# Where three activation buffers and three small tables lie in SBUF, in a two-block transformer kernel on one core

## The chip, the core and the metric

The program runs on one core of a Trainium2 chip. The metric is the device time of one execution in microseconds (us), as the median of several runs. Everything is held and computed in float32. Weights and activations that meet in a matmul are split into a high and a low part in a reduced format (`float32r`), and a product is made of three matmuls.

## What is computed

Two transformer blocks follow each other on 256 tokens of width 1024. The parts that matter here are the projections, all of them products of an activation with a large weight. In short:

```
# first block, two layers
for i in range(2):
    h = rmsnorm(x, mix_norm[i])
    p = h @ a_in   (layer 0: gated short convolution)  |  h @ b_in   (layer 1: stick-breaking attention)
    x = x + concat(y_main, y_mem) @ w_o[i]
    h = rmsnorm(x, ffn_norm[i])
    x = x + (silu(h @ w_gate[i]) * (h @ w_up[i])) @ w_down[i]       # inner width 2816
# second block: gated linear attention and spatial gating, context of 256 tokens
z = modulated_norm(x) @ w_in
x = x + g1 * ((sigmoid(ga) * (a @ w_br_a) + sigmoid(gb) * (ob @ w_br_b)) @ w_o)
x = x + g2 * ((gelu(conv3x3(h @ w_up_a)) * (h @ w_up_v)) @ w_down)   # inner width 2816
```

## The kernel before, in words

All weights come from one stream in HBM, cut into tiles of 128 x 1024 values. A tile is loaded into one of six `raw` buffers by the SyncE queue (L353), ScalarE makes its high part in one of four `w_hi` buffers (L889), and VectorE, or in the last stage GpSimd for half of the tiles, makes its low part in one of four `w_lo` buffers (L1411, L2111). TensorE then uses the tile in one of three ways:

- `tall` (L393): eight slices of 128 x 128 of the tile are the stationary operand, one after another; the moving operand is an activation of 256 columns, `H`, `Y`, `CX` or `HP`, and `mm3` (L381) makes three matmuls for each slice: high weight by high activation (L382), high by low (L383), low by high (L384). So a tile is 24 matmuls.
- `down` (L522): the same three matmuls for each of eight slices, with the moving operand `G`, one chunk of the hidden layer of a feed-forward stage. `G` has two sets that alternate.
- `wide` (L404): a slice of `H`, `Y` or `CX` is stationary, and the weight tile moves, with 256 or 512 columns (L387).

Each of `H` and `Y` is a pair of buffers, high and low, of 8192 bytes in each of the 128 partitions; the four `G` buffers have 1024 bytes each, a weight tile 4096. In the second block `H` and `Y` change names: `H2` is `Y`, `Y2` is `H` (L305). `CX` (the context's activation) and `HP` (258 columns, for the first two chunks of the last feed-forward stage) lie over the end of `ARENA`, the large work buffer; `W2S`, `CTX_LR` and `X_LR` belong to a small matmul in `log_decays` (L620), where a 96 x 256 activation moves over 96 x 128 weights.

Small tables are `MOD` (48 x 2 values, 384 bytes in a partition), which holds the modulation vectors, `GS` (3 x 8 values, 96 bytes), the scaled gains, and `small` (64 values, 256 bytes), for maxima, sums and statistics. VectorE and ScalarE read and write them.

SBUF is given out in the order of the `sb` calls of `build` (L209 to L249), without gaps but for rounding a buffer's size up to 32 bytes. Two calls make buffers that nothing uses: `phase` ahead of `H` and `whole` behind `G`, of `HALF_LINE` = 16 values, 64 bytes, each. The order of work on every engine is written out by hand, with semaphores between the engines; the places of the buffers don't enter into it.

Of the kernel before, what the change touches and what calls it, by code (L numbers as in the profile page):

```python
# [8 lines left out]
P = 128  # L9
D = 1024  # L10
KC = D // P
# [9 lines left out]
NMOD = 48  # L21
# [5 lines left out]
STACK = 96  # L27
EPS = 1e-6
RING = 4
HALF_LINE = 16  # L30
RAW = 6

F32 = mybir.dt.float32
# [163 lines left out]
def norm_low(tag, k):  # L197
    return ("norm_lo_dve", tag, k)
# [7 lines left out]
def build(nc, table, stream, vec, xT, memT, ctxT, c_rows, sq_consts, masks, scan_mask, sgu_bc, sgu_wT, gla_w2, out):  # L206
    pe, act, dve, pool, sp = nc.tensor, nc.scalar, nc.vector, nc.gpsimd, nc.sync
    with ExitStack() as ctx:
        def sb(name, shape, dt=F32):  # L209
            return ctx.enter_context(nc.sbuf_tensor(name, shape, dt))  # L210
# [5 lines left out]
        w_hi = [sb(f"w_hi{r}", [P, D], F32R) for r in range(RING)]  # L216
        w_lo = [sb(f"w_lo{r}", [P, D], F32R) for r in range(RING)]
        X = sb("X", [P, KC, T])
        sb("phase", [P, HALF_LINE])
        H = (sb("H_hi", [P, KC, T], F32R), sb("H_lo", [P, KC, T], F32R))  # L220
        Y = (sb("Y_hi", [P, KC, T], F32R), sb("Y_lo", [P, KC, T], F32R))
        G = [(sb(f"G_hi{i}", [P, T], F32R), sb(f"G_lo{i}", [P, T], F32R)) for i in range(2)]
        sb("whole", [P, HALF_LINE])
        SQ = sb("SQ", [P, KC, T])
        RS = sb("RS", [P, 2, T])
        GF = sb("GF", [P, T])
# [1 line left out]
        mask_sb = sb("mask_sb", [P, 3, P], U32)  # L228
        scan_m = sb("scan_m", [P, T])
        V = sb("V", [P, VEC_N])  # L230
        MOD = sb("MOD", [P, NMOD, 2])
        GS = sb("GS", [P, 3, KC])
        CROW = sb("CROW", [P, D])
        EPS_COL = sb("EPS_COL", [P, 1])[:]
        small = sb("small", [P, 64])
        W2 = sb("W2", [P, 512])
        LR = sb("LR", [P, T])
        CTX_LR = sb("CTX_LR", [P, T], F32R)
# [12 lines left out]
        def area(at, *shape):  # L251
            n = int(np.prod(shape))
            assert at + n <= 24832
            v = ARENA[:, at:at + n]
            if len(shape) == 1:
                return v
            names = "abc"[:len(shape)]
            return v.rearrange(f"p ({' '.join(names)}) -> p {' '.join(names)}",
                               **{names[i]: shape[i] for i in range(1, len(shape))})
# [14 lines left out]
        EXS, PTS = [area(8448, 8, T), area(11392, 8, T)], [area(10496, 4, 512), area(13440, 4, 512)]  # L274
        Y_MEM = [Y, H]
        NB = 3 * P
# [27 lines left out]

        H2, Y2 = Y, H  # L305
        RS_COLS = small[:, 32:34]
# [6 lines left out]

        SH1, SC1, G1, SH2, SC2, G2 = (lambda c, b=0, k=k: MOD[:, 8 * k + c, b:b + 1] for k in range(6))

# [56 lines left out]
        def pe_program():  # L372
# [8 lines left out]
            def mm3(o, wh, wl, xh, xl, start, stop):  # L381
                pe.matmul(o, wh, xh, start=start, stop=False, skip_group_check=True)  # L382
                pe.matmul(o, wh, xl, start=False, stop=False, skip_group_check=True)  # L383
                return pe.matmul(o, wl, xh, start=False, stop=stop, skip_group_check=True)  # L384
# [34 lines left out]
            def project(stage, count, h, release, side=None, ready=None, steps=1, order=range(KC)):  # L419
                assert n == AT[stage], (stage, n)  # L420
                for i in range(count):
                    b = bank_of(n)
                    claim(b)
                    tall(PS[:, b, 0:T], h, ready if i == 0 else None, order=order)
                    emptied[b] = [release(i)]
                    if side:
                        side.step(steps)

            def project_tokens(stage, width, h, banks, release, side, steps=1):
                assert n == AT[stage], (stage, n)  # L430
                claim(*banks)
                for part in range(KC * width // D):
                    wide([PS[:, b, 0:width] for b in banks], h, width, part)
                    if part == KC * width // D - 1:
                        for b in banks:
                            emptied[b] = [release]
                    side.step(steps)
# [84 lines left out]
            def down(l, j):  # L522
# [6 lines left out]
                for c in range(KC):  # L529
                    w = slice(c * P, (c + 1) * P)  # L530
                    last = mm3(PS[:, 4 + c // 2, (c % 2) * T:(c % 2 + 1) * T], w_hi[r][:, w], w_lo[r][:, w],
                               G[j % 2][0][:], G[j % 2][1][:], j == 0 and c % 2 == 0, j == FC - 1)
                    if j == FC - 1 and c % 2 and c != KC - 1:
# [216 lines left out]

            H_of = [H, H2, H2]

            def launch_norms():
                quarters("mix0", CSQ, 5)
                yield
                quarters("mem0")
                sum_quarters("mix0", 5)
                yield
                sum_quarters("mem0")
                yield  # L760
                pe.wait_ge(*past("rs", "mem0"))
                claim(4)
                for t in range(TT):
                    last = pe.transpose(PS[:, 4, t * P:(t + 1) * P], RS[:, 1, t * P:(t + 1) * P], IDENT)
                last.then_inc(*mark("rs_turned"))
                emptied[4] = [("rs_cols",)]
# [4 lines left out]
            side = Side(launch_norms())  # L771
            project("mem_k0", 2, Y, lambda i: ("km0", i), side, [norm_low("mem0", k) for k in range(KC)])
            project_tokens("mem_v0", 256, Y, (6, 7), ("vm0", 1), side)
            side.finish()

            project("a_q", 2, H, lambda i: ("qm", 0, i), None, [norm_low("mix0", k) for k in range(KC)])
            side = Side(memory_attention(0), context_rms())
            project("a_c", MC, H, lambda i: ("c", i), side)
            project("a_u", MC, H, lambda i: ("cu", i), side)
            project("a_b", MC, H, lambda i: ("gated", i), side)  # L780
            side.finish()
            y_ready = [("gated_lo", i) for i in range(MC)] + [("ma_lo", 0, c) for c in range(2)]
            project("w_o0", KC, Y, lambda i: ("added", 0, i), None, y_ready)
            ffn(0)

            def mix1_norm():
                quarters("mix1")
                yield
                sum_quarters("mix1")

            side = Side(mix1_norm())
            project("mem_k1", 2, Y, lambda i: ("km", 1, i), side, [norm_low("mem1", k) for k in range(KC)])
            project_tokens("mem_v1", 256, Y, (0, 1), ("vm", 1), side)
# [81 lines left out]
        def act_program():  # L875
# [133 lines left out]
            def hidden(l, j):  # L1009
                act.wait_ge(*past("hidden", l, j))  # L1010
                if j > 1:
                    act.wait_ge(*past("used", down_slot(l, j - 2)))
                act.activation(G[j % 2][0][:], up_product(j), ACT.Copy).then_inc(*mark("g_hi", l, j))

# [328 lines left out]
            act.wait_ge(*past("mod", 3))  # L1343
            act.activation(HP[0][:, :, T], MOD[:, 3 * KC:4 * KC, 0], ACT.Copy).then_inc(*mark("shift_hi"))
            project("w_o2", KC, left, then=residual_square(2, HP, lambda c: GS[:, 2, c:c + 1]))
            inverse_rms("res2")
# [57 lines left out]
        def dve_program():  # L1404
# [12 lines left out]
            def modulation(a):  # L1417
# [5 lines left out]
                if a < CTX_MODS:  # L1423
                    if a:
                        dve.wait_ge(*past("mod_dot", a - 1, 1))
                    dve.scalar_tensor_tensor(SQ[:, 0:4].rearrange("p c t -> p (c t)"), raw[at][:], 1.0, CTX_ROW,
                                             ALU.mult, ALU.mult,
                                             accum_out=MOD[:, a, 1:2]).then_inc(*mark("mod_dot", a, 1))
                    dve.wait_ge(*past("mod_dot", a, 1))
                dve.scalar_tensor_tensor(raw[at][:], raw[at][:], 1.0, CROW[:], ALU.mult, ALU.mult,  # L1430
                                         accum_out=MOD[:, a, 0:1]).then_inc(*mark("mod_dot", a, 0))
                if a % KC == KC - 1:
                    k, both = a // KC, 2 if a < CTX_MODS else 1
                    group, at = slice(KC * k, KC * k + KC), VEC_AT["b_ada"] + KC * k
                    dve.wait_ge(*past("mod_dot", a, 0))
                    dve.tensor_tensor(MOD[:, group, 0:both], MOD[:, group, 0:both],
                                      V[:, at:at + KC].unsqueeze(2).to_broadcast([P, KC, both]),
# [102 lines left out]
            def hidden_low(l, j):  # L1540
                dve.wait_ge(*past("g_hi", l, j))
                dve.tensor_tensor(G[j % 2][1][:], up_product(j), G[j % 2][0][:],  # L1542
                                  ALU.subtract).then_inc(*mark("g_lo", l, j))
# [88 lines left out]
            def scaled_gain(i, k, b, name):  # L1632
                at = VEC_AT[name]
                dve.scalar_tensor_tensor(GS[:, i], MOD[:, 8 * k:8 * k + 8, b], 1.0, V[:, at:at + 8], ALU.add,
                                         ALU.mult).then_inc(*mark("gs", i))
# [16 lines left out]
            def context_norm():  # L1652
# [4 lines left out]
                f = VEC_AT["final"]  # L1657
                dve.tensor_tensor(GS[:, 1], GS[:, 1], V[:, f:f + KC], ALU.mult).then_inc(*mark("gs_final"))
                yield from norms("ctx", CTX, lambda c: GS[:, 0, c:c + 1], ("ctx", RS_OF["ctx"]), CX,
                                 lambda c: SH1(c, 1), CTX)  # L1660
# [14 lines left out]
            def block1_end():  # L1675
# [10 lines left out]
                dve.wait_ge(*past("gs_final"))  # L1686
                yield from norms("norm1", X, lambda c: GS[:, 1, c:c + 1], ("norm1", RS[:, 1]), H2,
                                 lambda c: SH1(c))
# [333 lines left out]
            def merged_low(i):  # L2022
# [11 lines left out]
            project("w_o2", KC, residual(2, lambda c: G1(c)),  # L2034
                    then=residual_low(2, HP, lambda c: GS[:, 2, c:c + 1]))

# [267 lines left out]
```

## Time and profile before

| | us |
|---|---|
| median of 3 runs | 1138.15 |
| lowest, highest | 1137.81, 1138.23 |
| the profiled execution | 1140.99 |
| its span, first to last instruction | 1139.7 |
| TensorE matmuls busy | 1111.0 (97%) |
| TensorE weight loads busy | 1071.5 (94%) |
| VectorE busy | 837.0 (73%) |
| ScalarE busy | 627.6 (55%) |
| GpSimd busy | 146.3 (13%) |
| DMA, mean over the span | 193 GB/s |

Matmuls overlap: a record lasts some 280 ns, and the next matmul starts after less than half of that. Busy time of TensorE therefore says that it always had something in flight, and the pace is read from the starts. The weight load of the next matmul starts within some ns of the running one.

### The profile page before, as it was taken

The numbers are of one execution on the slowest core, as the hardware profiler recorded it, in microseconds if no ns is written. First come the engines' busy times: TensorE is split into PE (matmuls) and PEld (weight loads), VectorE is DVE, ScalarE is ACT, GpSimd is POOL, SyncE is SP. The second block draws the span as 40 slices with busy tenths as digits, with TensorE's granted clock in tenths as the row PEclk, the third lists the DMA queues.
The fourth block names the chain that finished last, engine by engine and source line by source line (L and its number), as shares of the span: only waits on it lengthen the run. The fifth ranks groups of instructions, "written<-read, shape, count | busy, mean of one in ns | idle before, by whom it ended". The sixth has DMA issues, their size and how long they took to land.

```text
span 1139.7 us, 21726 instructions
## 1 busy us (share of the span) xinstructions
PE 1111.0 (97%) x8918; PEld 1071.5 (94%) x8918; DVE 837.0 (73%) x1304; ACT 627.6 (55%) x951; POOL 146.3 (13%) x109
## 2 busy tenths in 40 slices
PE   7999999999899999999999999999999998999997
PEld 6989999999888899999999898989999998999996
DVE  5767687888876777777778677497646888778776
ACT  5655655444665655444444675666547465455553
POOL 0002201000000003100100000000000043344441
PEclk9999999999999999999999999999999998999999
DMA  8645578776544446798888645355445554565640
GB/s 326 224 156 177 173 246 284 243 256 207 201 131 148 130 134 200 234 291 275 283 263 297 229 163 189 107 185 154 143 126 174 183 167 133 182 187 184 190 162 37
DMA packets 60322, 221.49 MB, mean 194 GB/s; under 512 B 6720, under 2 KB 6976, under 8 KB 59840
## 3 DMA queue, kind: packets, MB, share of 16 engines
q1 hardware_dynamic: 59760, 218.53, 58.9%
q8 instruction: 71, 1.16, 0.4%
q10 hardware_dynamic: 288, 1.05, 0.3%
q0 software_dynamic: 176, 0.52, 0.1%
q14 instruction: 27, 0.22, 0.1%
HBM read 219.03 MB, written 1.05 MB: 193 GB/s over the span
## 4 chain that ended last, share of the span: by engine, by line
PE 84%; DVE 10%; ACT 3%; issue 2%; DMA 1%; SPq 0%; ACTq 0%; DVEq 0%
PE PS L382 24%; PE PS L383 23%; PE PS L384 23%; PE PS L387 13%; DVE w_lo L1411 3%; ACT w_hi L889 2%; DVE PS L2056 1%; DVE ARENA L1444 1%; DMA ARENA<-memT 1%; DVE SQ L1444 0%; DVE SQ L1719 0%; DVE H_lo L1454 0%; ACT ARENA L986 0%; DVE Y_lo L1454 0%; DVE Y_lo L1450 0%
## 5 line engine op out<-in xcount | busy, mean ns | idle before, releaser
L1411 DVE TENSOR_TENSOR w_lo<-raw,w_hi 128x1024 fp32r<-128x1024 f32 x324 | 397.1, 1228 | 160.9 <-ACT w_hi L889 160.2
L889 ACT ACTIVATE w_hi<-raw 128x1024 fp32r<-128x1024 f32 x356 | 371.5, 1054 | 129.4 <-PE PS L384 103.9
L382 PE MATMUL PS<-Y_hi,w_hi 128*128 128x256 f32 x1208 | 343.8, 285 | 9.1 <-DVE Y_lo L1450 3.3
L383 PE MATMUL PS<-Y_lo,w_hi 128*128 128x256 f32 x1208 | 340.5, 282 | 0.0
L384 PE MATMUL PS<-Y_hi,w_lo 128*128 128x256 f32 x1208 | 339.5, 281 | 0.0
L382 PEld LDWEIGHTS PS<-Y_hi,w_hi 128*128 128x128 f32 x1208 | 229.3, 190 | 13.0 <-issue 4.0
L383 PEld LDWEIGHTS PS<-Y_lo,w_hi 128*128 128x128 f32 x1208 | 229.3, 190 | 0.5 <-issue 0.2
L384 PEld LDWEIGHTS PS<-Y_hi,w_lo 128*128 128x128 f32 x1208 | 228.8, 189 | 0.0
L382 PE MATMUL PS<-H_hi,w_hi 128*128 128x256 f32 x768 | 217.2, 283 | 2.3 <-DVE w_lo L1411 1.4
L384 PE MATMUL PS<-H_hi,w_lo 128*128 128x256 f32 x768 | 214.4, 279 | 0.0
L383 PE MATMUL PS<-H_lo,w_hi 128*128 128x256 f32 x768 | 214.2, 279 | 0.0
L382 PE MATMUL PS<-G_hi,w_hi 128*128 128x256 f32 x528 | 148.3, 281 | 3.4 <-DVE G_lo L1542 3.4
L382 PEld LDWEIGHTS PS<-H_hi,w_hi 128*128 128x128 f32 x768 | 144.0, 187 | 7.4 <-issue 3.5
L383 PE MATMUL PS<-G_lo,w_hi 128*128 128x256 f32 x528 | 148.3, 281 | 0.0
L384 PE MATMUL PS<-G_hi,w_lo 128*128 128x256 f32 x528 | 147.9, 280 | 0.0
L383 PEld LDWEIGHTS PS<-H_lo,w_hi 128*128 128x128 f32 x768 | 144.2, 188 | 0.1
L384 PEld LDWEIGHTS PS<-H_hi,w_lo 128*128 128x128 f32 x768 | 144.1, 188 | 0.0
L382 PEld LDWEIGHTS PS<-G_hi,w_hi 128*128 128x128 f32 x528 | 100.0, 189 | 3.8 <-issue 3.8
L383 PEld LDWEIGHTS PS<-G_lo,w_hi 128*128 128x128 f32 x528 | 100.0, 189 | 0.0
L384 PEld LDWEIGHTS PS<-G_hi,w_lo 128*128 128x128 f32 x528 | 99.7, 189 | 0.0
L1031 ACT ACTIVATE GF<-GF 128x256 f32<-128x256 f32 x44 | 18.4, 418 | 140.0 <-DVE GF L1553 140.0
L2111 POOL TENSOR_TENSOR w_lo<-raw,w_hi 128x1024 fp32r<-128x1024 f32 x32 | 78.0, 2439 | 111.6 <-ACT w_hi L889 111.6
(251 smaller groups left out, 1391.4 us busy)
## 6 DMA issues: line engine op xcount, KB each, us to landing
raw<-stream SPq DMA_DIRECT2D x404, 512.0 KB, 4.2
ARENA<-memT SPq DMA_DIRECT2D x2, 512.0 KB, 7.7
X<-xT SPq DMA_DIRECT2D x1, 1024.0 KB, 11.3
ARENA<-ctxT SPq DMA_DIRECT2D x1, 1024.0 KB, 5.8
ARENA<-memT SPq DMA_DIRECT2D x1, 1024.0 KB, 8.0
outT<-ARENA SPq DMA_DIRECT2D x2, 512.0 KB, 2.6
CROW<-c_rows SPq DMA_DIRECT2D x1, 512.0 KB, 10.2
ARENA<-c_rows SPq DMA_DIRECT2D x1, 512.0 KB, 13.0
```

What stands on the lines that cost most here:

```text
L382: pe.matmul(o, wh, xh, start=start, stop=False, skip_group_check=True)
L383: pe.matmul(o, wh, xl, start=False, stop=False, skip_group_check=True)
L384: return pe.matmul(o, wl, xh, start=False, stop=stop, skip_group_check=True)
L387: return pe.matmul(o, w, x, start=start, stop=stop, skip_group_check=True)
L889: act.activation(w_hi[n % RING][:], raw[at][:], ACT.Copy).then_inc(*mark("hi", n))
L1031: act.activation(GF[:], GF[:], ACT.Silu).then_inc(*mark("silu", l, j))
L1411: dve.tensor_tensor(w_lo[n % RING][:], raw[raw_of("slot", n)][:], w_hi[n % RING][:], ALU.subtract).then_inc(*mark("lo_dve", n))
L1444: dve.scalar_tensor_tensor(via[:, c], src[:, c], g(c), rs[1], ALU.mult, ALU.mult).then_inc(*mark("norm", tag, c))
L2056: dve.scalar_tensor_tensor(conv_sum(j), IMGS[:, j % 2, r0:r0 + ROWS, c0:c0 + COLS], gain("fconv", j + t * FC), conv_sum(j), ALU.mult, ALU. ...
L2111: pool.tensor_tensor(w_lo[n % RING][:], raw[raw_of("slot", n)][:], w_hi[n % RING][:], ALU.subtract).then_inc(*mark("lo_pool", n))
```

## The change

The two unused buffers go. `MOD` moves from behind `V` to the place of `phase`, ahead of `H`; `GS` moves between `H` and `Y`; `small` between `Y` and `G`. No instruction, shape, semaphore or queue changes. `H` comes to lie 384 bytes from the weights' place within 512, `Y` 480 and `G` 224, where all three were at 64.

```diff
-HALF_LINE = 16
@@
         X = sb("X", [P, KC, T])
-        sb("phase", [P, HALF_LINE])
+        MOD = sb("MOD", [P, NMOD, 2])
         H = (sb("H_hi", [P, KC, T], F32R), sb("H_lo", [P, KC, T], F32R))
+        GS = sb("GS", [P, 3, KC])
         Y = (sb("Y_hi", [P, KC, T], F32R), sb("Y_lo", [P, KC, T], F32R))
+        small = sb("small", [P, 64])
         G = [(sb(f"G_hi{i}", [P, T], F32R), sb(f"G_lo{i}", [P, T], F32R)) for i in range(2)]
-        sb("whole", [P, HALF_LINE])
         SQ = sb("SQ", [P, KC, T])
@@
         V = sb("V", [P, VEC_N])
-        MOD = sb("MOD", [P, NMOD, 2])
-        GS = sb("GS", [P, 3, KC])
         CROW = sb("CROW", [P, D])
         EPS_COL = sb("EPS_COL", [P, 1])[:]
-        small = sb("small", [P, 64])
         W2 = sb("W2", [P, 512])
```

## Rows read from the trace of the kernel before

**Rows 1.** The page, busy time and share of the span by engine.
```profile
PE 1111.0 (97%) x8918; PEld 1071.5 (94%) x8918; DVE 837.0 (73%) x1304; ACT 627.6 (55%) x951; POOL 146.3 (13%) x109
```

**Rows 2.** TensorE's waits: waiting line, whom for, total us, times, longest.
```profile
PE PS L382 <- DVE G_lo L1542: 6.0, 3, 3.0
PE PS L382 <- DVE w_lo L1411: 4.7, 3, 3.3
PE PS L382 <- DVE Y_lo L1450: 3.3, 3, 2.4
```

**Rows 3.** Groups of matmuls by form: count, busy us, mean ns, idle before.
```profile
L383 PE MATMUL PS<-Y_lo,w_hi 128*128 128x256 f32 x1208 | 340.5, 282 | 0.0
L383 PE MATMUL PS<-H_lo,w_hi 128*128 128x256 f32 x768 | 214.2, 279 | 0.0
L383 PE MATMUL PS<-G_lo,w_hi 128*128 128x256 f32 x528 | 148.3, 281 | 0.0
...
L387 PE MATMUL PS<-w_hi,Y_lo 128*128 128x512 f32 x80 | 31.6, 395 | 0.0
...
L387 PE MATMUL PS<-w_hi,Y_lo 128*128 128x256 f32 x48 | 13.3, 276 | 0.0
...
L383 PE MATMUL PS<-CX_lo,w_hi 128*128 128x256 f32 x40 | 11.1, 277 | 0.0
```

**Rows 4.** Matmuls into PS, 130:230 us: ns min/median/max, first and last start.
```profile
L382 PE MATMUL PS<-H_hi,w_hi x196: 279/279/279, 129.8 to 229.8; 128*128 128x256 f32 x196
...
L382 PE MATMUL PS<-G_hi,w_hi x88: 279/279/279, 136.9 to 224.2; 128*128 128x256 f32 x88
```

**Rows 5.** Timeline of TensorE (start, us), then the window with PEclk, at 15 us.
```profile
15.09 0.41 PE L383 MATMUL PS<-Y_lo,w_hi 128*128 128x256 f32 x1
...
16.16 0.41 PE L382 MATMUL PS<-Y_hi,w_hi 128*128 128x256 f32 x1
...
15.30:16.40 1.10, 1.10 (x7) 1.10 (x7) 1.10 (x3) 1.10 (x3) 1.10 (x2) 0.50 1.02 406
```

**Rows 6.** Timeline of TensorE, G moving, at 283 us; 14 rows between.
```profile
282.77 0.28 PE L382 MATMUL PS<-G_hi,w_hi 128*128 128x256 f32 x1
...
284.47 0.28 PE L382 MATMUL PS<-G_hi,w_hi 128*128 128x256 f32 x1
```

**Rows 7.** Timeline of TensorE, CX moving, at 414 us; 43 rows between.
```profile
414.50 0.28 PE L382 MATMUL PS<-CX_hi,w_hi 128*128 128x256 f32 x1
...
419.49 0.28 PE L384 MATMUL PS<-CX_hi,w_lo 128*128 128x256 f32 x1
```

**Rows 8.** Timeline of TensorE, CTX_LR over W2S and the next start.
```profile
664.12 0.65 PE L387 MATMUL PS<-CTX_LR,W2S 96*128 96x256 f32 x4
664.61 0.28 PE L382 MATMUL PS<-Y_hi,w_hi 128*128 128x256 f32 x1
```

**Rows 9.** Timeline of TensorE, HP moving, at 933 us; 16 rows between.
```profile
933.34 0.28 PE L383 MATMUL PS<-HP,w_hi 128*128 128x258 f32 x1
...
935.41 0.28 PE L382 MATMUL PS<-HP,w_hi 128*128 128x258 f32 x1
```

**Rows 10.** Timeline of TensorE, weights moving over CX and Y; 6 and 11 between.
```profile
640.13 0.39 PE L387 MATMUL PS<-w_hi,CX_lo 128*128 128x512 f32 x1
...
641.73 0.40 PE L387 MATMUL PS<-w_lo,CX_hi 128*128 128x512 f32 x1
...
690.13 0.39 PE L387 MATMUL PS<-w_hi,Y_hi 128*128 128x512 f32 x1
...
692.93 0.39 PE L387 MATMUL PS<-w_hi,Y_hi 128*128 128x512 f32 x1
```

**Rows 11.** Windows: length, busy PE, PEld, DVE, ACT, POOL, PEclk, DMA, GB/s.
```profile
110.00:320.00 210.00, 206.13 (x1746) 204.82 (x1745) 166.43 (x253) 109.52 (x158) 22.88 (x28) 0.99 0.71 226
...
950.00:1139.70 189.70, 178.92 (x1488) 176.27 (x1486) 138.90 (x259) 93.11 (x149) 73.22 (x30) 0.98 0.48 156
```

**Rows 12.** The page, costliest groups: low part of a weight tile.
```profile
L1411 DVE TENSOR_TENSOR w_lo<-raw,w_hi 128x1024 fp32r<-128x1024 f32 x324 | 397.1, 1228 | 160.9 <-ACT w_hi L889 160.2
```

## The prediction

> **What bounds the kernel now.** I read the page's shares first: TensorE's matmuls are busy for 97% of the span, and no other engine is near that [rows 1]. Then the waits of TensorE: the three largest come to 14.0 of 1139.7 us [rows 2], and none below them is above 3.2 us. So the end is set by how fast TensorE takes one matmul after another, and not by a producer. The groups of matmuls by form say which ones: Y is the moving operand of 3 x 1208 matmuls, H of 3 x 768, G of 3 x 528, in all 7512 matmuls of 256 columns; 240 more move 512 columns of a weight over a stationary slice of Y, and 144 move 256 [rows 3].
>
> The busy time of these groups is of no use for their price, since a matmul's record (280 ns) overlaps the next two. What counts is the distance from start to start. In the 100 us of one undisturbed stretch of the first feed-forward stage, L382 starts 196 + 88 times between 129.8 and 229.8 us; 283 triples in 100.0 us are 353.4 ns each, **117.8 ns for one matmul** [rows 4]. 7512 x 117.8 ns = 885 us: four fifths of the span is this one number. It is not the streaming time. At 15 to 16 us the granted clock was 0.50, the lower level of 1.2 GHz, and there the same matmul came every 1.07/5 = 214 ns [rows 5]; half of that, 107 ns, is what 256 columns take at the full clock. So 10.8 ns of each 117.8 are lost to something that shows at the full rate alone.
>
> **What the losses have to do with places.** The change adds and removes no instruction; it moves buffers. Counting sizes from X on (all buffers up to X are whole multiples of 512 bytes), and writing each place as its distance modulo 512 from the weights: before, H, Y and G stand at 64, CX at 448 (that is -64), HP's columns at 448 + 8k (high part) and 8k (low part), and W2S, CTX_LR and X_LR all at 448, so 0 from one another. While a matmul streams its moving operand, the next weights are loaded; that pair of reads is what a distance can touch. Four places of the trace give a price per distance:
> - 64 (H, Y, G): 117.8 ns [rows 4], but at 283 us 15 intervals of G at the same distance take 1.70 us, **113.3 ns** [rows 6]. A distance thus has more than one steady pace, and a stretch keeps the one that it fell into. How rare the quick one is can be read from the mean durations: 276 ns belong to 113.3, 279 to 280 to 117.8 ns, and the groups of L383 have 279 to 282 [rows 3, 4, 6].
> - 448 (CX moving): 44 intervals in 4.99 us, **113.4 ns** [rows 7]; the mean duration of its whole group, 277 ns, is near 276 [rows 3].
> - 0 (CTX_LR moving over W2S): four matmuls and the step to the next take 0.49 us, **122 ns** each [rows 8].
> - mixed and off every multiple of 64 (HP, 258 columns): 17 intervals in 2.07 us, 121.8 ns, less 0.8 ns for two more columns, **121.0 ns** [rows 9].
> With a weight as the moving operand of 512 columns, Y as the stationary one gives 12 intervals in 2.80 us, 233 ns, and CX gives 7 in 1.60 us, 229 ns [rows 10].
> The pace does depend on the place: the operations, shapes and types of the first two are equal.
>
> **The change part by part.**
> - *H from 64 to 384*, 2304 matmuls. 384 is three times 128: if what repeats is 128 bytes, H now lies like the weights, and the nearest row is the distance 0, 122 ns [rows 8]. That is +4.2 ns x 2304 = +9.7 us. If what repeats is 512 bytes, the nearest row is 448 with 113.4 ns [rows 7]: -4.4 x 2304 = -10.1 us.
> - *Y from 64 to 480*, 3624 matmuls. 480 is 32 bytes short of distance 0, and 32 past 448. Its neighbours are 122 and 113.4 ns; the only row off the multiples of 64 is HP's 121.0 [rows 9], and HP's high part passes 480 itself. I take it: +3.2 x 3624 = +11.6 us. The ends are -15.9 and +15.2 us.
> - *G from 64 to 224*, 1584 matmuls, 32 short of a multiple of 128 (and of 256) like Y. +3.2 x 1584 = +5.1 us; ends -7.0 and +6.7 us.
> - *Y as stationary operand* (L387, distance from 448 to 32) and *CX* (448 to 320, the same modulo 128): rows of 229 and 233 ns are 4 ns apart [rows 10], so 240 matmuls are worth 1 us either way, the 144 of 256 columns and the 120 of CX no more than 8.6 ns x 264 = 2.3 us. I take 0. HP goes through a whole set of places before and after: 0. W2S and its operands stay at 0 from one another.
> - *MOD, GS, small* in new places, and SQ and what follows it moved by 96 to 608 bytes: VectorE, ScalarE and GpSimd touch them with the same instructions. In the two longest feed-forward stretches VectorE is busy 166 of 210 us and 139 of 190 us [rows 11], so a few per cent on its operations would be covered by TensorE; uncovered is only what follows the last matmul, under 1% of the span, where a per cent more or less is 0.1 us. Two pads of 64 bytes are gone; they cost no time.
> - The order of waits stays. A slower TensorE gives VectorE and ScalarE more time, so +1 ns on a matmul is +1 ns on the span. A faster one draws on their slack: a weight tile needs 1.2 us of VectorE for its low part [rows 12] against 24 x 113.4 ns = 2.7 us of TensorE, so a gain would come through too, save in the last stage, where [rows 11] leaves 139 of 190.
>
> Sum: 9.7 + 11.6 + 5.1 = +26.4 us on the profiled execution's 1141.0 us (its span is 1139.7): 1167.4 us. That execution stands 2.8 us above the median of 1138.15, so the forecast is **1164.6 us**.
>
> The page "TensorE: Matmul & The Clock Gate" of the Trainium skill (Part 2, step 1) speaks against any effect: matmul data and weights are read through two independent SBUF ports, so that loading the next weights takes no bandwidth from the running matmul; by its gap formula (Back-to-back issue gap) 256 columns would follow each other every 109 ns. The trace disagrees with it at 117.8 and at 113.4 ns for equal operations. It is kept below as the rival of no effect.
>
> **The rivals.**
> - *Distance repeats at 512 and 448 is the good side.* H (-128) and Y (-32) lie on both sides of -64, whose row shows 113.4 ns [rows 7]; CX and Y as stationary operands, -64 and 64 apart from the weights, also differ [rows 10], which a period of 128 can't give. Then the pace of all three falls to 113.4: 7512 x 4.4 = 33 us, 1105 us. With G (far from both) left where it is, 1112; with only H and G better, 1121. Against it: CX also lies more than 120 KB away from the weights and H, Y and G don't, so its pace may be a matter of region; [rows 6] show 113.3 at distance 64, so that what I call the better distance may be one more fall of the dice; and 480 is nearer to 0 than any place of before.
> - *Gains and losses cancel.* Y slower by 11.6 to 15.2, H and G faster by 10.1 and 7.0: from -5 to -2 us, 1133 to 1136. It needs the two distances to act in opposite ways.
> - *The distance does nothing*, and the paces are set by how each stretch starts [rows 6]. Then about nothing changes, 1138 us. Against it: stretches of H, Y and G fall to 117.8 nearly always, CX mostly to 113.4. By the rule of the page above, the result would be this one as well.
> - *All three fall to 122 ns or beyond*, the row of distance 0: 7512 x 4.2 = +31.6, 1170 us. This is the top of my own case.
>
> **How the numbers follow.** Slower as worked out, between half of the sum and the last rival (1151 to 1172): 0.54. Faster, 1105 to 1133: 0.35. No effect, or cancelled to within 0.2% (2.3 us, about what a measurement of this kernel can tell from no change): 0.10; the last 0.01 goes to slower. A difference in pace of 0.3 ns is already 2.3 us, so "same" is narrow. Faster by over 0.2%: 0.35; within: 0.10; slower: 0.55. As both signs hold a good part, the range has to reach into both: from 1107 to 1172 us; it leaves out the whole gain of 33 us and more, and paces beyond 122. The likeliest case's own range is 1151 to 1172.
>
> **What would show it.** In the profile after: the distance from start to start in a long stretch of the first feed-forward stage, for H and G, and in the second one for Y. By my case H near 122, Y and G near 121, and the modelled duration of these matmuls up from 279 ns by 2 to 4; by the first rival 113.4 and 276 ns. CX should stay at 113.4 if 128 bytes is the period, and may change if it is 512. W2S and CTX_LR, whose mutual distance stays 0, should stay at 122. VectorE's and ScalarE's durations should be unchanged. I am wrong if Y's pace falls below 117.8, since Y alone carries half of the matmuls; wrong in mechanism if the times move while the paces don't.

## The result and the profile after

| | before | after |
|---|---|---|
| median | 1138.19 us | 1144.49 us |
| lowest, highest | 1137.79, 1140.35 | 1143.49, 1147.61 |
| ratio, 95% interval | | 1.0057 [1.0043, 1.0071] |
| the profiled execution, its span | 1140.99, 1139.7 | 1147.61, 1146.3 |

The change makes the kernel slower by 6.3 us; the forecast was 26.4 us. The sign held, and so did the wide range; the likeliest case's own range, 1151 to 1172 us, did not. Of the mechanism, the distance to the weights held; the period of 128 bytes and the prices did not.

The page of the kernel after, busy time by engine, and the waits of TensorE that answer to [rows 2] (line numbers are 3 lower than before, so L382 to L384 are now L379 to L381):

```profile
PE 1120.8 (98%) x8918; PEld 1079.4 (94%) x8918; DVE 837.4 (73%) x1304; ACT 627.8 (55%) x951; POOL 146.0 (13%) x109
```
```profile
PE PS L379 <- DVE G_lo L1539: 5.2, 3, 2.8
PE PS L379 <- DVE Y_lo L1447: 3.6, 4, 2.5
...
PE PS L379 <- DVE w_lo L1408: 2.5, 3, 1.5
```

Against [rows 1] TensorE alone is busy for longer, by 9.8 us; the other engines have the same work in the same time. The waits for `G_lo` and `w_lo` are even shorter in this profile, 7.7 us where they were 10.7 [rows 2]. So the kernel is slower within its matmuls. The groups by form (count, busy us, mean ns, idle before), which answer to [rows 3] and [rows 12]:

```profile
L380 PE MATMUL PS<-Y_lo,w_hi 128*128 128x256 f32 x1208 | 341.0, 282 | 0.0
L380 PE MATMUL PS<-H_lo,w_hi 128*128 128x256 f32 x768 | 217.2, 283 | 0.0
L380 PE MATMUL PS<-G_lo,w_hi 128*128 128x256 f32 x528 | 149.3, 283 | 0.0
...
L384 PE MATMUL PS<-w_hi,Y_lo 128*128 128x512 f32 x80 | 31.6, 395 | 0.0
...
L380 PE MATMUL PS<-CX_lo,w_hi 128*128 128x256 f32 x40 | 11.2, 279 | 0.0
```
```profile
L1408 DVE TENSOR_TENSOR w_lo<-raw,w_hi 128x1024 fp32r<-128x1024 f32 x324 | 397.1, 1228 | 163.9 <-ACT w_hi L886 163.6
```

VectorE takes 1228 ns for a low part, as before. H has gone from 279 to 283 ns, G from 281 to 283, CX from 277 to 279, and Y hardly moves. But these durations are modelled from what follows and say little; the starts do. Matmuls into PS in the stretch of [rows 4], and for Y in the second block (count, ns min/median/max, first and last start):

```profile
L379 PE MATMUL PS<-H_hi,w_hi x192: 279/285/287, 129.9 to 229.9; 128*128 128x256 f32 x192
...
L379 PE MATMUL PS<-G_hi,w_hi x88: 277/280/285, 136.8 to 225.2; 128*128 128x256 f32 x88
```
```profile
L380 PE MATMUL PS<-Y_lo,w_hi x187: 277/281/285, 499.9 to 597.2; 128*128 128x256 f32 x187
...
L380 PE MATMUL PS<-G_lo,w_hi x95: 277/281/285, 503.8 to 599.7; 128*128 128x256 f32 x95
```

In the first, 280 starts of L379 are 279 triples in 100.0 us: 119.5 ns a matmul, against 117.8 [rows 4]. In the second, 282 starts of L380 are 281 triples in 99.8 us: 118.4 ns; the kernel before had 284 starts there, 283 triples in 100.0 us, 117.8 ns:

```profile
L383 PE MATMUL PS<-Y_lo,w_hi x188: 280/280/280, 499.8 to 599.8; 128*128 128x256 f32 x188
...
L383 PE MATMUL PS<-G_lo,w_hi x96: 280/280/280, 500.9 to 596.6; 128*128 128x256 f32 x96
```

The way to read the rows is the same for every kernel below: add the counts of the two operands on one line, take one off, and divide the time between the first and the last start.

The mean time from start to start over all stretches, from the starts of all matmuls to the ns, gives the loss by operand. The distances of operands are bytes modulo 512 from the weights, as in the prediction; in the rows for 256 and 512 columns a weight moves, and its distance is counted from the stationary slice:

| operand | count | distance | ns before | ns after | us |
|---|---|---|---|---|---|
| H moving | 2304 | 64 to 384 | 117.35 | 119.19 | +4.2 |
| Y moving | 3624 | 64 to 480 | 117.73 | 118.32 | +2.1 |
| G moving | 1584 | 64 to 224 | 117.51 | 118.36 | +1.3 |
| 256 columns of a weight over Y | 144 | 448 to 32 | 113.7 | 116.96 | +0.5 |
| CX moving | 120 | 448 to 320 | 114.5 | 117.75 | +0.4 |
| 512 columns of a weight over CX | 96 | 64 to 192 | 229.15 | 233.3 | +0.4 |

That is 8.9 us; the 512 columns over Y stay at 233.2. H has two paces here: of the 79 tiles of 24 matmuls that no wait interrupts, 42 average 118.5 to 118.9 ns and 37 average 119.9 to 120.0. The span grew by 6.6 us: in this pair of profiles the shorter waits give 3.0 us back, and the 0.7 us left over are less than what executions of one kernel differ by (1143.49 to 1147.61 us).

### The profile page after: what moved, and what is told of

The parts are those of the page before. It is cut to its first block, busy times and chain, and to the rows that moved or that the text cites. A ratio compares the mean times of both kernels' runs of the same rounds, so it can differ in the third digit from the quotient of the medians.

```text
span 1146.3 us, 21726 instructions
## 1 busy us (share of the span) xinstructions
PE 1120.8 (98%) x8918; PEld 1079.4 (94%) x8918; DVE 837.4 (73%) x1304; ACT 627.8 (55%) x951; POOL 146.0 (13%) x109
## 4 chain that ended last, share of the span: by engine, by line
PE 83%; DVE 11%; ACT 3%; issue 2%; DMA 1%; SPq 0%; ACTq 0%; DVEq 0%
PE PS L379 23%; PE PS L380 23%; PE PS L381 23%; PE PS L384 13%; DVE w_lo L1408 3%; ACT w_hi L886 2%; DVE PS L2053 2%; DMA X<-xT 1%; DVE ARENA L1441 1%; DVE SQ L1441 0%; DVE SQ L1716 0%; DVE H_lo L1451 0%; ACT ARENA L983 0%; DVE Y_lo L1451 0%; DVE Y_lo L1447 0%
## 5 line engine op out<-in xcount | busy, mean ns | idle before, releaser
L1408 DVE TENSOR_TENSOR w_lo<-raw,w_hi 128x1024 fp32r<-128x1024 f32 x324 | 397.1, 1228 | 163.9 <-ACT w_hi L886 163.6
L379 PE MATMUL PS<-Y_hi,w_hi 128*128 128x256 f32 x1208 | 345.2, 286 | 8.0 <-DVE Y_lo L1447 3.6
L380 PE MATMUL PS<-Y_lo,w_hi 128*128 128x256 f32 x1208 | 341.0, 282 | 0.0
L381 PE MATMUL PS<-Y_hi,w_lo 128*128 128x256 f32 x1208 | 340.9, 282 | 0.0
L379 PEld LDWEIGHTS PS<-Y_hi,w_hi 128*128 128x128 f32 x1208 | 229.2, 190 | 12.3 <-issue 4.4
L380 PEld LDWEIGHTS PS<-Y_lo,w_hi 128*128 128x128 f32 x1208 | 229.4, 190 | 0.5 <-issue 0.2
L381 PEld LDWEIGHTS PS<-Y_hi,w_lo 128*128 128x128 f32 x1208 | 229.3, 190 | 0.0
L379 PE MATMUL PS<-H_hi,w_hi 128*128 128x256 f32 x768 | 220.0, 286 | 1.9 <-DVE w_lo L1408 1.0
L380 PE MATMUL PS<-H_lo,w_hi 128*128 128x256 f32 x768 | 217.2, 283 | 0.0
L381 PE MATMUL PS<-H_hi,w_lo 128*128 128x256 f32 x768 | 217.1, 283 | 0.0
L379 PE MATMUL PS<-G_hi,w_hi 128*128 128x256 f32 x528 | 149.3, 283 | 2.3 <-DVE G_lo L1539 2.3
L379 PEld LDWEIGHTS PS<-H_hi,w_hi 128*128 128x128 f32 x768 | 145.2, 189 | 6.7 <-issue 3.1
L380 PE MATMUL PS<-G_lo,w_hi 128*128 128x256 f32 x528 | 149.3, 283 | 0.0
L381 PE MATMUL PS<-G_hi,w_lo 128*128 128x256 f32 x528 | 149.1, 282 | 0.0
L380 PEld LDWEIGHTS PS<-H_lo,w_hi 128*128 128x128 f32 x768 | 145.2, 189 | 0.1
L381 PEld LDWEIGHTS PS<-H_hi,w_lo 128*128 128x128 f32 x768 | 145.2, 189 | 0.0
L379 PEld LDWEIGHTS PS<-G_hi,w_hi 128*128 128x128 f32 x528 | 100.4, 190 | 2.7 <-issue 2.7
L381 PEld LDWEIGHTS PS<-G_hi,w_lo 128*128 128x128 f32 x528 | 100.4, 190 | 0.0
L380 PEld LDWEIGHTS PS<-G_lo,w_hi 128*128 128x128 f32 x528 | 100.4, 190 | 0.0
L2108 POOL TENSOR_TENSOR w_lo<-raw,w_hi 128x1024 fp32r<-128x1024 f32 x32 | 77.7, 2429 | 113.7 <-ACT w_hi L886 113.7
```

The source lines that it names most:

```text
L1408: dve.tensor_tensor(w_lo[n % RING][:], raw[raw_of("slot", n)][:], w_hi[n % RING][:], ALU.subtract).then_inc(*mark("lo_dve", n))
L2108: pool.tensor_tensor(w_lo[n % RING][:], raw[raw_of("slot", n)][:], w_hi[n % RING][:], ALU.subtract).then_inc(*mark("lo_pool", n))
```

## The experiments

The theory after the result: only the distance between the moving operand and the weights counts, modulo 256 bytes. That each distance allows a few steady paces, of which a stretch keeps the one that it falls into, was added when the first layouts had run; until then 192 was expected to be quick throughout. Rivals: the operand's own address; the tables and work buffers that moved; a period of 128 or of 512 bytes; the region of SBUF. All kernels compute the whole reference; only places differ. The first four layouts share a chip and 18 executions of the kernel before; the one with only H at 384 and the three for the period share another chip and 13 executions; the one with only Y and G moved, the one at 448 and the changed kernel once more share a third chip and 13 more.

One rival needs no run. VectorE and ScalarE write weight tiles while TensorE reads, and might slow it. In the profile of the kernel before, the steps through which VectorE is idle average 117.6 ns (1504 steps of H, Y and G), those with VectorE at work 117.6 ns too (5694); with ScalarE idle or at work it is 117.6 both times, and in the layout at 0 all four means are 119.9 ns. So the pace does not hang on what these engines do meanwhile.

### The tables moved, H, Y and G left at 64

```diff
-        sb("phase", [P, HALF_LINE])
+        V = sb("V", [P, VEC_N])
         H = ...
...
-        sb("whole", [P, HALF_LINE])
@@
-        V = sb("V", [P, VEC_N])
```

> H, Y and G stay at 64 as before, but the two pads are gone (V, 1600 bytes, lies ahead of H) and ARENA, CX, HP, W2S lie exactly where the change puts them (320). Theory A: H, Y and G at 117.8 ns, CX (now 64 modulo 256) at 117.8 instead of 113.4 ns, 120 matmuls, and the wide ones over CX: under 1 us more than before, 1138 to 1139.5 us. Theory C (moved tables and work buffers cost the time): the 6 us of the change come back, 1144 us.

Measured: 1139.02 us against 1138.98, ratio 0.9997 [0.9981, 1.0013]. `ARENA`, `CX`, `HP` and `W2S` lie at 320 here as in the changed kernel, `SQ` and the tables at new places. H, Y and G keep 117.3 to 117.8 ns. So moved tables and work buffers are worth nothing outside -2.2 to +1.5 us, though the tables do not lie here where the change puts them, and no pad is needed to have 64. CX alone, now at 320, has lost its 113.4 and goes at 117.77 ns.

### H, Y and G at 192

As above, with `pair_small` (128 bytes) also put between `V` and `H`:

```diff
-        sb("phase", [P, HALF_LINE])
+        V = sb("V", [P, VEC_N])
+        pair_small = sb("pair_small", [P, 2, 2, GH * TT])
...
-        sb("whole", [P, HALF_LINE])
@@
-        V = sb("V", [P, VEC_N])
@@
-        pair_small = sb("pair_small", [P, 2, 2, GH * TT])
```

> H, Y and G lie at 192 from the weights' place (V and a table of 128 bytes ahead of H, no padding); CX, HP and W2S stay at the distances of before. Theory A: the pace of a matmul depends on the distance between moving operand and weights modulo 256. Before, CX at 448 (192 modulo 256) went at 113.3 ns a matmul, so H, Y and G go at 113.3 instead of 117.8 ns: 7512 x 4.4 = 33 us less, 1138 becomes 1105 us. Theory B: the quick pace of CX came from the region of memory in which it lies, more than 120 KB from the weights. Then H, Y and G stay at 117.8 or go like any other offset, 118 to 119 ns: 1138 to 1146 us. Theory C: the time follows the tables and work buffers that move with the change, not H, Y and G: SQ moves here too, so some us either way, but no 33.

Measured: 1134.0 us (1124.6 to 1137.8, 9 runs), ratio 0.9949 [0.9919, 0.9978]: faster than the kernel before, but by 5 us, where theory A expected 33. Matmuls into PS of the profiled execution (1127.21 us), at 500 and at 1000 us:

```profile
L381 PE MATMUL PS<-Y_lo,w_hi x191: 281/281/281, 499.8 to 598.0; 128*128 128x256 f32 x191
...
L381 PE MATMUL PS<-G_lo,w_hi x93: 281/281/281, 505.1 to 599.8; 128*128 128x256 f32 x93
```
```profile
L380 PE MATMUL PS<-Y_hi,w_hi x192: 276/276/277, 1002.5 to 1097.4; 128*128 128x256 f32 x192
...
L380 PE MATMUL PS<-G_hi,w_hi x103: 276/276/276, 999.8 to 1099.7; 128*128 128x256 f32 x103
```

The same instructions on the same buffers: 283 triples in 100.0 us, 117.8 ns, and 294 triples in 99.9 us, 113.3 ns. The whole stretch of 1559 matmuls that holds the first window is at 117.8, that of some 1250 with the second at 113.3. One stretch changes within, at a step of 180 ns (timeline, start and duration in us):

```profile
231.02 0.28 PE L382 MATMUL PS<-H_hi,w_lo 128*128 128x256 f32 x1
231.14 0.34 PE L380 MATMUL PS<-H_hi,w_hi 128*128 128x256 f32 x1
231.32 0.28 PE L381 MATMUL PS<-H_lo,w_hi 128*128 128x256 f32 x1
231.43 0.28 PE L382 MATMUL PS<-H_hi,w_lo 128*128 128x256 f32 x1
```

Two steps of 114 and 113 ns stand ahead of it, 115 and then 118 and 117 behind it; the first 960 or so matmuls of the stretch of 1247 were quick, the rest are not. Of the 266 tiles that no wait interrupts, 148 are quick, that is, average under 114.5 ns (in the kernel before, at distance 64, 10 of 267). Y, H and G average 115.7, 115.1 and 115.6 ns, which is 15.7 us less than before; the span is 13.8 us shorter. The nine executions scatter over 13 us, the 18 of the kernel before over 9; that fits paces that are drawn anew each time, but only one of the nine was profiled, so it is not shown.

### All three at 0, the distance of the row that priced H

```diff
-        sb("phase", [P, HALF_LINE])
...
-        sb("whole", [P, HALF_LINE])
+        sb("whole", [P, 32])
```

> H, Y and G at 0, the same place as the weights within 512; SQ and all that follows exactly as before. Theory A: 0 is a place of its own in the period; CTX_LR over W2S at distance 0 went at 119 to 122 ns, so 7512 x (1.4 to 4.2) = 10 to 32 us more: 1149 to 1170 us. If the distance were indifferent: 1138 us. If the period were 128 bytes, H at 384 of the changed kernel (118.7 to 120 ns) would be the same place, and all three would go at about 119 ns: 1147 us.

Measured in one execution: 1152.26 us, 1.2% above. Matmuls into PS at 130 us:

```profile
L381 PE MATMUL PS<-H_hi,w_hi x191: 283/283/283, 129.8 to 229.9; 128*128 128x256 f32 x191
...
L381 PE MATMUL PS<-G_hi,w_hi x88: 283/283/283, 138.8 to 227.7; 128*128 128x256 f32 x88
```

278 triples in 100.1 us: 120.0 ns, here and in nearly every other tile. The distance 0 is the worst uniform one of all that were run, and it costs 2.2 ns, not the 4.2 of [rows 8]. Nothing but H, Y and G moved here, so the 13 us are theirs. With a weight moving over a stationary slice, 0 is the best: 512 columns over Y take 228.6 ns, where 233.2 were taken before.

### The weights moved, the operands' addresses kept

```diff
+        MOD = sb("MOD", [P, NMOD, 2])
         w_hi = ...
...
-        sb("phase", [P, HALF_LINE])
+        pair_small = sb("pair_small", [P, 2, 2, GH * TT])
+        sb("phase", [P, 16])
...
-        sb("whole", [P, HALF_LINE])
+        sb("whole", [P, 16])
@@
-        MOD = sb("MOD", [P, NMOD, 2])
@@
-        pair_small = sb("pair_small", [P, 2, 2, GH * TT])
```

The weights stand 384 bytes further on, H, Y and G at the same addresses modulo 512 as before, hence at distance 192.

> The weights are moved by 384 bytes and H, Y and G keep their address within 512 of before; their distance from the weights becomes 192, and so does CX's. Theory A (the distance between the two counts): 113.3 ns for H, Y, G and CX, about 1105 us. Rival D (the address of the moving operand itself within a line counts): H, Y and G stay at 117.8 ns, 1138 us.

Measured in one execution: 1128.77 us, 10.2 below the kernel before, a third of what theory A expected. At 500 and at 1000 us:

```profile
L382 PE MATMUL PS<-Y_hi,w_hi x192: 281/281/281, 501.3 to 599.8; 128*128 128x256 f32 x192
...
L382 PE MATMUL PS<-G_hi,w_hi x92: 281/281/281, 499.9 to 594.2; 128*128 128x256 f32 x92
```
```profile
L382 PE MATMUL PS<-Y_hi,w_hi x196: 276/276/276, 999.9 to 1098.8; 128*128 128x256 f32 x196
...
L382 PE MATMUL PS<-G_hi,w_hi x99: 276/276/276, 1001.2 to 1099.8; 128*128 128x256 f32 x99
```

283 triples in 99.9 us (117.7 ns) and 294 in 99.9 us (113.3 ns), the two paces of 192 again, with 120 of 268 tiles quick. What counts is the distance to the weights, not the operand's own address.

### Only H at 384

```diff
-        sb("phase", [P, HALF_LINE])
+        MOD = sb("MOD", [P, NMOD, 2])
         H = ...
+        GS = sb("GS", [P, 3, KC])
+        sb("phase", [P, 24])
         Y = ...
...
-        sb("whole", [P, HALF_LINE])
+        sb("whole", [P, 8])
@@
-        MOD = sb("MOD", [P, NMOD, 2])
-        GS = sb("GS", [P, 3, KC])
```

> Only H goes to the place of the change (384, with MOD ahead of it); Y and G are back at 64, ARENA and CX where they were before. Theory A (each buffer pays for its own distance): H at 118.7 to 120.0 ns as in the changed kernel, Y and G at 117.8, so H's share of the loss alone, 2304 x 1.8 = +4 us: 1142 to 1143 us. Rival: the loss comes with Y and G, which hold 5208 of the 7512 matmuls; then this one is at 1138 to 1139 us.

Measured: 1140.05 us against 1139.39, ratio 1.0008 [0.9996, 1.002], short of the 1142 to 1143 us expected. Matmuls into PS at 130 us:

```profile
L383 PE MATMUL PS<-H_lo,w_hi x194: 279/281/287, 130.0 to 229.8; 128*128 128x256 f32 x194
...
L383 PE MATMUL PS<-G_lo,w_hi x88: 278/279/280, 137.5 to 225.2; 128*128 128x256 f32 x88
```

281 triples in 99.8 us, 118.4 ns, where the changed kernel had 119.5 in the same stretch. H at 384 costs 1.3 ns here, 2.9 us by the mean of 118.62; the ratio leaves room for 2.3 us at most, so either part of it is taken up elsewhere or the other executions had less of it, which one profile doesn't show.

### Only Y at 480 and G at 224

```diff
-        sb("phase", [P, HALF_LINE])
+        sb("phase", [P, 16])
         H = ...
+        MOD = sb("MOD", [P, NMOD, 2])
+        sb("phase_y", [P, 8])
         Y = ...
+        small = sb("small", [P, 64])
         G = ...
-        sb("whole", [P, HALF_LINE])
+        sb("whole", [P, 8])
@@
-        MOD = sb("MOD", [P, NMOD, 2])
@@
-        small = sb("small", [P, 64])
```

> The complement of h384: H stays at 64 and CX at 448 as before; Y goes to 480 and G to 224 as in the changed kernel. Prices by the changed kernel's own paces: Y 118.32 - 117.73 = +0.59 ns x 3624 = +2.1 us, G 118.36 - 117.51 = +0.85 x 1584 = +1.3 us, the 144 narrow ones over the stationary Y +0.5: sum +3.9 us, ratio 1.0034. With the +0.9 us of h384 that would be only +4.8 of the +6.3 us measured for the change. Rival: H's slow stretch of 120.0 ns in the first feed-forward stage (h384 alone had 118.4 there) is brought by G at 224 between the H matmuls; then H, though at 64, would be above 117.8 ns in that stretch here as well.

Measured: 1142.27 us against 1139.36, ratio 1.0032 [1.0018, 1.0046], as expected. At 130 us and at 500 us:

```profile
L385 PE MATMUL PS<-H_hi,w_lo x196: 279/279/279, 129.7 to 229.8; 128*128 128x256 f32 x196
...
L385 PE MATMUL PS<-G_hi,w_lo x88: 277/280/285, 137.2 to 224.5; 128*128 128x256 f32 x88
```
```profile
L384 PE MATMUL PS<-Y_lo,w_hi x186: 277/280/285, 500.0 to 599.8; 128*128 128x256 f32 x186
...
L384 PE MATMUL PS<-G_lo,w_hi x96: 277/280/285, 500.4 to 596.6; 128*128 128x256 f32 x96
```

283 triples in 100.1 us (117.9 ns) with H at 64 beside G at 224: G's place does not slow H, so H's 120.0 ns in the changed kernel was not brought by G's place alone. 281 triples in 99.8 us (118.4 ns) for Y and G. Y and G thus cost 2.9 us and H alone 0.7. Together that is 3.6 of the 6.3 us. By the profiles, CX and the weights over CX, which neither layout moves, are worth another 0.8, and H at its slower pace 1.3 more than in the layout with only H moved; that makes 5.7, an accounting and not a run.

### The changed kernel once more

> The changed kernel once more, for its paces. If a distance fixes the set of paces and the entry picks one, H (384) in the first feed-forward stage may be at 118.4 or 118.7 ns this time where the first profile had 120.0, worth 1.5 us; Y (480) and G (224) stay at 118.3. If the layout as a whole fixes it, H is at 120.0 there again. Time 1143.5 to 1147.6 us.

Measured: 1144.84 us. Matmuls into PS at 130 us, and for both profiles of the changed kernel the window from 0 to 37 us (columns as in [rows 11]), this one's last:

```profile
L379 PE MATMUL PS<-H_hi,w_hi x194: 279/281/285, 130.0 to 230.0; 128*128 128x256 f32 x194
L379 PE MATMUL PS<-G_hi,w_hi x88: 277/280/285, 137.5 to 225.3; 128*128 128x256 f32 x88
```
```profile
0.00:37.00 37.00, 31.77 (x217) 26.89 (x218) 22.77 (x42) 22.48 (x41) 1.98 (x7) 1.00 0.87 320
```
```profile
0.00:37.00 37.00, 29.82 (x209) 26.38 (x210) 21.86 (x40) 21.57 (x40) 1.97 (x7) 0.95 0.85 311
```

H and G take 118.6 ns together in the stretch that had 119.5: 281 triples in 100.0 us. Over the whole kernel H is at 118.68 instead of 119.19, while Y (118.32) and G (118.28) repeat. So 384 has two paces, near 118.7 and at 120.0, and the layout does not choose between them. The waits for `G_lo` and `w_lo` are 9.3 us here, where the first profile had 7.7. The windows show what else differs between two executions: the first had a mean granted clock of 1.00, the level of 2.4 GHz, the second 0.95, part of it at 1.2 GHz as in the kernel before [rows 5], with 8 matmul records fewer in the same time.

### Three more layouts, for the period

H at 32 with Y and G at 96; H at 160 with Y and G at 128; H at 208 with Y and G at 176 (off the multiples of 32, by slices of one larger buffer, with CX at 64). The first in short:

```diff
-        sb("phase", [P, HALF_LINE])
+        sb("phase", [P, 8])
         H = ...
+        sb("phase_y", [P, 16])
         Y = ...
...
-        sb("whole", [P, HALF_LINE])
+        sb("whole", [P, 8])
```

> H at 32; Y and G at 96; all else as before. If the pattern repeats every 128 bytes (theory A128), 96 is the same place as 224 and 480: Y and G at 118.3 ns, and H at 32 something of its own between 118 and 120. If it repeats every 256 only (theory A256), 96 lies between 64 (117.8 ns) and 128 (118.7 to 120) and can have a pace that differs from 118.3.

> H at 160; Y and G at 128; CX as before. A128: 128 is the place of 0, so Y and G at 120.0 ns (5208 x 2.2 = +11.5 us), and H at 160 like H at 32 of the run beside it. A256: 128 is the place of 384, 118.7 to 120.0 ns, and 160 differs from 32, nearer to the quick 192: 1138 to 1148 us.

> H at 208, Y and G at 176, 16 bytes to either side of 192, where about half of the tiles went at 113.3 and half at 117.8 ns. Theory E: the share of quick tiles rises and falls smoothly around 192; a side on which all of them go at 113.3 would give 1105 to 1120 us. Rival: a start off the multiples of 32 costs more, as with HP (121 ns): 1138 to 1160 us. CX lies at 64 here, in the far region: if the distance sets its pace and the region doesn't, it goes at 117.8 ns, and at 113.4 if the region does.

Measured in one execution each: 1150.06, 1149.62 and 1147.18 us, against 1139.39; the second is above the 1138 to 1148 expected for a period of 256. Matmuls into PS at 500 us, of the first and of the second:

```profile
L383 PE MATMUL PS<-Y_hi,w_hi x183: 278/278/283, 499.8 to 599.9; 128*128 128x256 f32 x183
...
L383 PE MATMUL PS<-G_hi,w_hi x96: 278/280/283, 501.2 to 598.8; 128*128 128x256 f32 x96
```
```profile
L382 PE MATMUL PS<-Y_hi,w_hi x183: 281/281/281, 499.8 to 599.9; 128*128 128x256 f32 x183
...
L382 PE MATMUL PS<-G_hi,w_hi x96: 281/281/281, 501.6 to 599.2; 128*128 128x256 f32 x96
```

Both are 278 triples in 100.1 us, 120.0 ns. In the third, CX at distance 64 goes at 117.79 ns although it lies as far off as ever: its 113.4 was a matter of distance, not of region.

### All three at 448

```diff
-        sb("phase", [P, HALF_LINE])
+        MOD = sb("MOD", [P, NMOD, 2])
+        sb("phase", [P, 16])
         H = ...
...
-        sb("whole", [P, HALF_LINE])
+        sb("whole", [P, 16])
@@
-        MOD = sb("MOD", [P, NMOD, 2])
```

> H, Y and G at 448, the very place that CX had before (MOD and a pad ahead of H, a pad behind G; CX stays at 448). If what repeats is 256 bytes, 448 is 192: half of the tiles near 113.3 ns and half at 117.8, Y and G near 115.6, ratio near 0.995 (0.991 to 0.998). If what repeats is 512 bytes and 448 is the good side proper, nearly all at 113.3: -33 us, ratio 0.971. If the period is 128, as 64: 117.8 and ratio 1.000. 240 wide matmuls over Y get the distance 64 and 229 instead of 233 ns, a gain of 1 us, in each case but the last.

Measured: 1132.32 us (1126.5 to 1133.8, 4 runs) against 1139.36, ratio 0.9925 [0.9898, 0.9952]. At 500 and at 1000 us:

```profile
L383 PE MATMUL PS<-Y_lo,w_hi x188: 281/281/281, 499.8 to 599.8; 128*128 128x256 f32 x188
...
L383 PE MATMUL PS<-G_lo,w_hi x96: 281/281/281, 501.2 to 597.0; 128*128 128x256 f32 x96
```
```profile
L383 PE MATMUL PS<-Y_lo,w_hi x199: 276/276/276, 999.8 to 1099.7; 128*128 128x256 f32 x199
...
L383 PE MATMUL PS<-G_lo,w_hi x96: 276/276/276, 1005.2 to 1097.4; 128*128 128x256 f32 x96
```

283 triples in 100.0 us (117.8 ns) and 294 in 99.9 us (113.3 ns): the same two paces as at 192, and again mixed, with means of 115.7 (Y), 116.5 (H) and 116.2 ns (G). 448 is the good place that CX had, but it is good less than half of the time (110 of 266 tiles). By the median this is the fastest layout that ran more than once, together with 192; their intervals overlap.

### What the runs give together

Paces of 256 columns by distance modulo 256, all from starts, as means of tiles:

| distance | from | ns |
|---|---|---|
| 0 | H, Y, G | 120.0 |
| 32 | H | 116.7, 117.8 or 118.4 |
| 64 | H, Y, G, CX; CX at 320 | 117.8; H, Y and G seldom 113.3 |
| 96 | Y, G | 119.6 to 120.2 |
| 128 | Y, G; H at 384 | 118.3 to 119.0, or 120.0 |
| 160 | H | 117.3 or 118.5 to 118.9 |
| 176 | Y, G | 119.2 on average |
| 192 | H, Y, G, also at 448; CX at 448 | 113.3 or 117.8, about even |
| 208 | H | 116.7, 117.4 or 119.1 |
| 224 | G; Y at 480 | 118.3 |

The pairs that are 256 apart agree: 64 and 320, 192 and 448, 224 and 480, 128 and 384. Pairs 128 apart don't: 96 has 119.9 and 224 has 118.3; 64 is quick in 4% of its tiles and 192 in about half. So the period is 256 bytes, as far as these pairs go; 256 itself was not tried against 0, and 128 against 384, 224 against 480 compare different buffers. A weight of 512 columns moving over a stationary slice shows it too: 233.3 ns with CX at 192 and with Y at 448, 229 with CX at 64 and 230.0 with Y at 64.

## Why the prediction was right in sign and wrong in size

The sign was right, but in part by luck: H was called slower because 384 was put with 0 by a period that does not hold, and Y and G because of a row from another place. The result, 6.3 us, lies between 2.3 us and half of the sum (13.2), where the prediction had left a chance of 0.01.

- **What bounds the kernel**: right. The loss is in the starts of the matmuls, VectorE's 1228 ns stayed, and moved tables cost nothing that can be measured (the layout with 64 kept: 0.9997).
- **The distance to the weights acts**: right, and shown: moving the weights under unmoved operands gives the paces of the new distance.
- **H, +4.2 ns for +9.7 us**: the direction was right, both parts of the price failed. The period is 256 and not 128, so 384 is not the distance 0; and 0 itself is 120.0 ns over thousands of matmuls, not the 122 of [rows 8]. There four steps were read from starts rounded to 0.01 us, as 0.49 us; to the ns they are 124, 121, 120 and 117, 0.482 us, 120.5 ns each. Their expected constancy failed too: in the changed kernel the same four average 119.3. Measured: +1.3 to +1.8 ns, 2.9 to 4.2 us.
- **Y, +3.2 ns for +11.6 us, and G, +5.1 us**: the step that failed most is the row of `HP` [rows 9], taken as their price. Seventeen intervals of matmuls with 258 columns, at a place that changes from one to the next, were taken as the price of 480 and 224, because no other row was off the multiples of 64. Measured: +0.6 ns for Y and +0.8 for G, 2.1 and 1.3 us; alone they make 1.0032. With the terms as measured the sum would have been 8.9 us, CX and the stationary operands included.
- **CX and the stationary operands, taken as 0**: 1.3 us, all three terms on the slow side; it fits within the 3.3 us that stood there as bound, though the 96 matmuls over CX had not been counted. The 0.5 us of the 256 columns may be a draw: unmoved at 448, they took 116.4 ns in the layout with the tables moved, not 113.7. CX's fall from 113.4 to 117.75 was the sign named for a period other than 128.
- **+1 ns on a matmul is +1 ns on the span**: nearly. The matmuls lost 8.9 us and the span 6.6; at 192 they gained 15.7 and the span 13.8. That shorter waits are what cushions the loss is not shown: those for `G_lo` and `w_lo` fell from 10.7 to 7.7 us in the first pair, but they are 9.3 us in the second profile of the changed kernel, and 9.0 us with H, Y and G at 64 and nothing slower.
- **The first rival** (448 is the good side) was true of 448, as the last layout shows. It failed for the change since 384 and 480 are not near enough: 32 bytes to either side, at 160 and 224, no tile is quick. Its price was too high as well: at 448 less than half of the tiles fall to 113.3, 7 us and not 33.
- **No effect, the paces set by how a stretch starts**: half true. A stretch picks one of the paces, mostly at its start, but the distance sets which ones there are. By the rule of the Trainium skill's page "TensorE: Matmul & The Clock Gate" (Part 2, step 1: loading weights takes nothing from the running matmul) all layouts would be alike; the runs disagree, with 1129 to 1152 us for layouts that differ in places alone.
- **All three at 122 or beyond**: no layout reached it; the slowest was 120.0 ns and 1152 us.

Left open: what picks the pace at the start of a stretch, what in the weights' place acts (their load into TensorE is the one reader that runs beside every matmul, but no run separates it), whether a short wait always draws anew as the 180 ns did once, and what in the memory the 256 bytes are. No run here tells these apart.

## What to carry to other kernels

When one pair of operands meets thousands of times, read the distance from start to start per stretch, not the mean duration, and count how many steady paces a place shows before pricing a move. A price for such an effect has to come from a long stretch of the same form; four matmuls, or a form with other columns, gave two to five times the true value. Steps in a timeline are rounded to 10 ns, and over four matmuls that alone made 2 ns of error. A layout is worth trying where the moving operand lies 192 bytes from the weights modulo 256, but its gain of 0.5 to 0.75% is made of paces that vary by stretch, so it needs several executions to be seen.

## What the runs showed of the hardware

- Back-to-back matmuls of 256 columns ran at paces from 113.3 to 120.0 ns at the full clock (113.3, 116.7, 117.8, 118.3, 118.7, 119.2 and 120.0 the commonest), by the distance between moving operand and weights modulo 256 bytes, where half of the time at 1.2 GHz is 107 [rows 5], whether or not VectorE and ScalarE were at work.
- A distance can have two steady paces (113.3 and 117.8 at 192; 118.7 and 120.0 at 384), kept for up to 1559 matmuls; two profiles of the changed kernel had different ones in the same stretch, and one layout took from 1124.6 to 1137.8 us.
- With 512 columns of a weight over a stationary activation the order of places is another one, by the weight's distance from the slice modulo 256: 228.6 ns at 0, 229 to 230 at 64, 233.3 at 192 and at 32.
